# Expert choice in a three-block network: fewer candidate places, a fused look-up, and 62 pieces of the first expert layer in 512-column products

## The chip, the cores and the metric
One NeuronCore of a Trainium2 chip. The metric is the device time of one execution in microseconds (us), the median of several runs of the same program. Engines are named as in the profile: PE (TensorE matrix products), PEld (its weight loads), DVE (VectorE), ACT (ScalarE), POOL (GpSimd), SP (SyncE, which issues the loads).

## The reference, cut to what matters
The network has three blocks over 256 tokens of width 1024. The change lies in the expert layer (PEER) that ends the second block. For each token there are 8 heads; each head picks 16 of 16384 experts through two lists of 128 keys:

```python
q = (xt @ w_q).reshape(T, PEER_HEADS, PEER_QDIM)
s1 = jnp.einsum('thd,hkd->thk', q[..., :half], keys1)
s2 = jnp.einsum('thd,hkd->thk', q[..., half:], keys2)
v1, i1 = lax.top_k(s1, PEER_TOPK)
v2, i2 = lax.top_k(s2, PEER_TOPK)
cand = (v1[..., :, None] + v2[..., None, :]).reshape(T, PEER_HEADS, 256)
cidx = (i1[..., :, None] * 128 + i2[..., None, :]).reshape(T, PEER_HEADS, 256)
sv, pos = lax.top_k(cand, PEER_TOPK)
eidx = jnp.take_along_axis(cidx, pos, axis=-1)
gw = jax.nn.softmax(sv, axis=-1)
act = jnp.einsum('td,thkd->thk', xc, jnp.take(u_tab, eidx, axis=0))
hact = jax.nn.gelu(act, approximate=False) * gw
y = jnp.einsum('thk,thkd->td', hact, jnp.take(v_tab, eidx, axis=0))
```

## The kernel before, in words
The kernel gathers no rows of `u_tab`. It multiplies all 16384 rows with all 256 tokens, takes the Gelu of all products, builds a weight for every (expert, token) pair that is zero where the expert was not chosen, multiplies the two, and multiplies the result with all of `v_tab`. `peer` exists once for each engine (L1228 PE, L2419 DVE, L3504 ACT; POOL's part starts at L1496).

A **piece** is 128 rows of a weight matrix with all 1024 inputs, a tile of 128 x 1024. Each number is carried as a high part (rounded to fp32r) and a low part (the rest). SP loads a chunk of two pieces (1 MB) into one of three raw slots; ACT makes the high part of each piece (L2896), DVE (L1543) or POOL (L1431, `lower`) subtracts to get the low part. The parts lie in a ring of four, so the high part of piece n can be made when PE has read piece n-4; a raw slot is loaded again when both its pieces have their low parts. In every engine's program `weights()` steps to the next piece: ACT makes high parts up to three pieces ahead, DVE low parts up to two pieces ahead, except those listed in `on_pool` (L379), which POOL makes in a row of its own.

`peer`'s stretch of 128 pieces of `u_tab` has two stages, cut at piece `SELECTED`.

- **Search stage**, pieces 0 to 71. PE makes each piece's products in the narrow form (`tile_mms`, L580): 8 x (high weights with high inputs, high weights with low inputs) and 8 x low weights with high inputs, 24 products of 256 columns, each with its own weight load. Two pieces share a PSUM bank of the four in `main`. ACT takes the Gelu of two pieces from PSUM (L3547). DVE runs the choice of experts beside it, as a generator, `select()` (L2474), which `shared` lets go on by 1750 columns with each piece: 32 rounds of five instructions (L2453 to L2458: largest 8, their places, strike them out, next 8, their places) on 128 scores; per token half the 256 sums of 16 x 16 candidates (L2480) and eight rounds of five on 256 columns; shifts and masks that split a place into its row and column (L2487, L2489); a look-up for each of the two index lists and token halves that compares places with 0 to 15 (L2495, 2048 columns), multiplies with the indices (L2499, eight times 256 columns) and sums (L2504). ACT takes the exponential (L3560), DVE divides (L2514 to L2518). POOL makes the low part of every odd piece.
- **Weighing stage**, from piece 72. PE turns the selection around (L1259), and from piece 74 to 126, in 64 groups of four tokens, DVE, ACT and POOL build one-hot tiles (in raw slot 2, which is kept free for that), PE multiplies them into the weights (L1268), and DVE multiplies these with the Gelu (L2560) or copies them where the Gelu is not there yet (L2561). `groups_of` spreads the groups over the pieces.

The other form of product in the kernel is `wide` (L742). High and low inputs lie beside each other, so one product of 512 columns makes both parts with one weight load (L747), and 8 products of 256 columns add the low weights (L746). A piece then takes a whole bank, whose two halves are still to be added. The queries of this layer are made so: ACT copies one half (L3517), DVE adds the other (L2433).

Of the kernel before, what the change touches and what calls it, by code (L numbers as in the profile page):

```python
# [7 lines left out]
F32 = mybir.dt.float32  # L8
# [13 lines left out]
SELECTED = 72  # L22
FIRST_HOT, LAST_HOT = 74, 126
# [4 lines left out]
LOW = -3.0e38  # L28
# [263 lines left out]

BAND = [(o, i) for o in range(10) for i in range(10)
# [18 lines left out]
class Program:  # L312


    def __init__(self, nc, d, out, mem, ctx, marks, known):
# [63 lines left out]
        self.on_pool = [0] + [self.u_first + n for n in range(1, SELECTED, 2)] + [self.next_four("m3") - 1]  # L379
# [129 lines left out]
def tensor_engine(k):  # L509
# [718 lines left out]
    def peer(prev):  # L1228
# [43 lines left out]
        for n in range(128):  # L1272
            if n % 2 == 0:
                b = main.take(pe, ("pr.u", n))
            m, hi, lo = weights()
            o = n % 2 * 256
            ins = tile_mms(ps[:, b, o:o + 256], m, hi, lo, X, 0, 8, True, True, rx)
            ins.then_inc(k.piece_read, 1)
            if n % 2:
                k.full["pr.u", n - 1] = k.piece_read, m + 1  # L1280
            if n == SELECTED:
                selected()
            for g in groups_of(n):
                weigh(g)
# [132 lines left out]
def gpsimd_engine(k):  # L1417
# [80 lines left out]
    for n in range(1, SELECTED, 2):  # L1498
        lower(k.u_first + n)
# [28 lines left out]
def vector_engine(k):  # L1528
# [893 lines left out]
    def peer(prev):  # L2422
# [17 lines left out]
        pd = k.AR[:, B0 + 2048:B0 + 2560].bitcast(U32).rearrange("p (j s n) -> p j s n", s=2, n=128)  # L2440
        pf = k.AR[:, B0 + 2560:B0 + 3072].rearrange("p (j s n) -> p j s n", s=2, n=128)
        sel = k.AR[:, B0 + 3072:B0 + 3840].rearrange("p (w j n) -> p w j n", w=3, n=128)
        cand = k.AR[:, B0 + 4096:B0 + 6144].rearrange("p (h a b) -> p h a b", a=16, b=16)
        eq = k.AR[:, B0 + 6144:B0 + 8192]
        e3 = eq.rearrange("p (n a) -> p n a", a=16)
        e4 = eq.rearrange("p (h k a) -> p h k a", k=16, a=16)
# [23 lines left out]
        def select():  # L2470
# [6 lines left out]
            yield 256  # L2477
            for j in range(2):
                v.wait_ge(*k.dma["spilled"].need("x"))
                chained(te.tensor_tensor(cand, bc(v_[:, j, 0].unsqueeze(3), [128, 8, 16, 16]),  # L2480
                                         bc(v_[:, j, 1].unsqueeze(2), [128, 8, 16, 16]), ALU.add))
                yield 2048
                for h in range(8):
                    yield from best(sv[:, j, h], pu[:, j, h], cand[:, h].rearrange("p a b -> p (a b)"))
            for j in range(2):
                pj = pu[:, j].rearrange("p h k -> p (h k)")
                chained(te.tensor_single_scalar(pd[:, j, 0], pj, 4, ALU.logical_shift_right))  # L2487
                yield 128
                chained(te.tensor_single_scalar(pd[:, j, 1], pj, 15, ALU.bitwise_and))  # L2489
                yield 128  # L2490
            chained(te.tensor_copy(k.AR[:, B0 + 2560:B0 + 3072], k.AR[:, B0 + 2048:B0 + 2560].bitcast(U32)))
            yield 256
            for j in range(2):
                for sd in range(2):
                    chained(te.tensor_tensor(e3, bc(pf[:, j, sd].unsqueeze(2), [128, 128, 16]),  # L2495
                                             bc(k.iota[:, 0:16].unsqueeze(1), [128, 128, 16]), ALU.is_equal))
                    yield 2048
                    for h in range(8):
                        ins = te.tensor_tensor(e4[:, h], e4[:, h], bc(ifl[:, j, sd, h].unsqueeze(1), [128, 16, 16]),  # L2499
                                               ALU.mult)  # L2500
                        if h == 7:
                            chained(ins)
                        yield 256
                    chained(te.tensor_reduce(sel[:, sd, j], e3, AX.X, ALU.add))  # L2504
# [10 lines left out]
            yield 256  # L2515
            chained(te.reciprocal(st[:, 80:96], st[:, 64:80]))
            yield 16
            te.tensor_tensor(sel[:, 2].rearrange("p j (h k) -> p (j h) k", k=16), svn,  # L2518
                             bc(st[:, 80:96].unsqueeze(2), [128, 16, 16]), ALU.mult).then_inc(*step.mark("pr.sel"))
            yield 256  # L2520
# [32 lines left out]
        def weighed(g, m):  # L2553

            v.wait_ge(*full["pr.w", g])
            if not weighed_before(m - 2):
                v.wait_ge(*main.gone(("pr.u", m - 2)))
# [321 lines left out]
def scalar_engine(k):  # L2879
# [624 lines left out]
    def peer(prev):  # L3504
# [34 lines left out]
        def taken(f):  # L3539

            t = weighed_before(f) * 4
# [8 lines left out]
        for n in range(128):  # L3550
# [6 lines left out]
            if n == SELECTED - 2:  # L3557
                w = k.AR[:, B0 + 1536:B0 + 1792]
                a.wait_ge(*s["vec"].need(("pr.sv", 1)))
                act(w, w, ACT.Exp).then_inc(*s["act"].mark("pr.exp"))  # L3560
# [5 lines left out]
            if n % 2 and n < 127:  # L3566
                taken(n - 1)
# [379 lines left out]
```

## Time and profile before
| what | value |
|---|---|
| median of 3 runs | 2816.77 us (2816.17 to 2816.78) |
| span of the profiled execution, first to last instruction | 2814.9 us |
| what lies around the span, median less span | 1.9 us |
| busy in the span: PE, DVE, ACT, POOL | 2800.3, 1952.1, 1624.4, 345.9 us |

The page gives the profiled execution's span; its whole time is taken as one of the runs listed. How to read the rows: in the timeline the first number is the start from the span's beginning, the second the time from there to the end of the last of the instructions merged in the row, both in us; in brackets stands how long the engine was idle before it and whom it waited for. PE instructions overlap, so its pace is read from starts. A piece of the narrow form has one row of eight low-weight products (L589), one of the wide form a row of eight at L746.

### The profile page before, as it was taken

Reading aid. Unit: us, or ns where it says so; the run is one execution under the profiler, and the core shown is the slowest. Engines: PE = TensorE matmul, PEld = TensorE weight load, DVE = VectorE, ACT = ScalarE, POOL = GpSimd, SP = SyncE. Lnnn points to the kernel's source line nnn. Section 1 sums busy time; section 2 is a strip of 40 time slices with the busy share of each in tenths; the row PEclk is TensorE's granted clock in tenths of the full one; section 3 lists DMA queues with packets and bytes.
Section 4 is the critical chain, followed back from the end, with each engine's and each line's share of the span. In section 5 each row is a group of like instructions: output and inputs, shape, how many; then the busy total and the mean of one; then the engine's idle time right before and its main releaser. Section 6 shows DMA issues by size and latency. Waiting matters only on the chain.

```text
span 2814.9 us, 42397 instructions
## 1 busy us (share of the span) xinstructions
PE 2800.3 (99%) x16834; PEld 2485.0 (88%) x16834; DVE 1952.1 (69%) x3377; ACT 1624.4 (58%) x2784; POOL 345.9 (12%) x314
## 2 busy tenths in 40 slices
PE   9999999999999999999999999999999999999999
PEld 7888888888988888899889999999888889988997
DVE  6657765776676676768866998677555566766775
ACT  6544655755665564566745445776555555655663
POOL 0000000000010002000002445894000000000000
PEclk9999999999999999999999999999999999999999
DMA  7554556466436555445164554434555574536454
GB/s 229 191 178 159 181 194 227 135 202 221 148 124 194 202 189 181 135 156 187 61 224 166 183 182 160 136 131 161 193 192 193 194 246 137 180 110 209 147 195 149
DMA packets 270485, 491.25 MB, mean 175 GB/s; under 512 B 10880, under 2 KB 181248, under 8 KB 261584
## 3 DMA queue, kind: packets, MB, share of 16 engines
q1 hardware_dynamic: 268864, 480.08, 51.3%
q0 software_dynamic: 1424, 8.45, 0.8%
q8 instruction: 135, 2.21, 0.3%
q14 instruction: 62, 0.51, 0.1%
HBM read 486.41 MB, written 2.10 MB: 174 GB/s over the span
## 4 chain that ended last, share of the span: by engine, by line
PE 94%; DVE 4%; ACT 1%; issue 0%; DMA 0%; POOL 0%; DVEq 0%; POOLq 0%; ACTq 0%
PE ps L659 41%; PE ps L747 11%; PE ps L589 8%; PE ps L585 8%; PE ps L586 8%; PE ps L746 6%; PE ps L606 3%; PE ps L1268 2%; DVE halves L1543 1%; PE ps L1303 1%; PE ps L544 1%; DVE AR L2499 1%; PE ps L952 0%; PE ps L1322 0%; DVE AR L2495 0%
## 5 line engine op out<-in xcount | busy, mean ns | idle before, releaser
L2896 ACT ACTIVATE halves<-raw 128x1024 fp32r<-128x1024 f32 x828 | 870.1, 1058 | 695.5 <-PE ps L659 413.7
L1543 DVE TENSOR_TENSOR halves<-raw,halves 128x1024 fp32r<-128x1024 f32 x790 | 952.9, 1227 | 190.6 <-ACT halves L2896 187.4
L659 PE MATMUL ps<-halves,XX 128*128 128x512 f32 x2628 | 611.6, 391 | 0.4
L659 PEld LDWEIGHTS ps<-halves,XX 128*128 128x128 f32 x2628 | 489.9, 188 | 102.5 <-DVE XX L1581 1.0
L585 PE MATMUL ps<-XX,halves 128*128 128x256 f32 (+1 forms) x1960 | 486.1, 286 | 0.0
L586 PE MATMUL ps<-XX,halves 128*128 128x256 f32 (+1 forms) x1960 | 480.3, 283 | 0.0
L659 PE MATMUL ps<-halves,R 128*128 128x512 f32 x1908 | 439.9, 390 | 0.1
L659 PEld LDWEIGHTS ps<-halves,R 128*128 128x128 f32 x1908 | 356.7, 188 | 73.9 <-issue 0.6
L586 PEld LDWEIGHTS ps<-XX,halves 128*128 128x128 f32 (+1 forms) x1960 | 375.4, 192 | 0.1
L585 PEld LDWEIGHTS ps<-XX,halves 128*128 128x128 f32 (+1 forms) x1960 | 375.0, 191 | 0.1
L747 PE MATMUL ps<-XX,halves 128*128 128x512 f32 x1344 | 338.4, 393 | 0.6 <-DVE XX L1581 0.6
L747 PEld LDWEIGHTS ps<-XX,halves 128*128 128x128 f32 x1344 | 241.7, 189 | 44.5 <-ACT halves L2896 0.9
L589 PE MATMUL ps<-XX,halves 128*128 128x256 f32 (+1 forms) x1960 | 275.3, 283 | 0.2 <-DVE halves L1543 0.2
L589 PEld LDWEIGHTS ps<-XX,halves 128*128 128x128 f32 (+1 forms) x1960 | 252.7, 192 | 0.4 <-DVE halves L1543 0.4
L746 PEld LDWEIGHTS ps<-XX,halves 128*128 128x128 f32 x1344 | 183.2, 190 | 13.4 <-issue 0.4
L746 PE MATMUL ps<-XX,halves 128*128 128x256 f32 x1344 | 187.5, 282 | 0.1
L1426 POOL TENSOR_TENSOR st<-st 128x1 f32<-128x1 f32 x44 | 25.3, 574 | 1182.0 <-DVE st L1608 1001.9
L1431 POOL TENSOR_TENSOR halves<-raw,halves 128x1024 fp32r<-128x1024 f32 x38 | 97.0, 2552 | 435.3 <-ACT halves L2896 435.3
L1558 DVE TENSOR_TENSOR XX<-AR,XX 128x256 fp32r<-128x256 f32 x127 | 53.9, 426 | 137.9 <-ACT XX L3579 137.9
L1509 POOL TENSOR_SCALAR raw<-iota,xsel 128x128 f32<-128x128 f32 x128 | 137.5, 1081 | 34.5 <-PE ps L1268 22.4
L1807 DVE TENSOR_TENSOR AR<-AR,ps 128x256 f32<-128x256 f32 x164 | 68.5, 421 | 81.1 <-ACT AR L3096 81.1
L3096 ACT ACTIVATE AR<-ps 128x256 f32<-128x256 f32 x164 | 61.3, 375 | 89.4 <-PE ps L747 88.0
(390 smaller groups left out, 3180.8 us busy)
## 6 DMA issues: line engine op xcount, KB each, us to landing
raw<-in_w_ffn_in SPq DMA_DIRECT2D x88, 1024.0 KB, 5.1
raw<-in_w_in SPq DMA_DIRECT2D x74, 1024.0 KB, 5.3
raw<-in_uT SPq DMA_DIRECT2D x64, 1024.0 KB, 4.9
raw<-in_peer_v SPq DMA_DIRECT2D x64, 1024.0 KB, 4.9
raw<-in_w_ffn_out SPq DMA_DIRECT2D x44, 1024.0 KB, 4.9
raw<-in_w_up SPq DMA_DIRECT2D x24, 1024.0 KB, 5.8
raw<-in_mlstm_w_in SPq DMA_DIRECT2D x12, 1024.0 KB, 5.2
raw<-in_w_down SPq DMA_DIRECT2D x12, 1024.0 KB, 4.9
```

Of the source, the lines that this page charges most:

```text
L585: mm(o[:, ts], hi[:, q, 0:M], xh[:, k0 + q, ts], start=first and q == 0, stop=False)
L586: mm(o[:, ts], hi[:, q, 0:M], xl[:, k0 + q, ts], start=False, stop=False)
L589: ins = mm(o[:, ts], lo[:, q, 0:M], xh[:, k0 + q, ts], start=False, stop=last and q == a - 1)
L606: ins = mm(ps[:, bs[j], :].rearrange("p (a b) -> p a b", b=128), act[q == 2][:, t, j * 128:(j + 1) * 128], k.halves[:, 0:4, q % 2, t * 128 ...
L659: ins = mm(ps[:, bs[j * (width // 512) + h], :], xv[:, k0 + t, j * 128:(j + 1) * 128], wv[:, t, h * 512:(h + 1) * 512], start=first and q ...
L746: mm(o[:, 0:256], lo[:, p, :], X[0][:, p, :], start=False, stop=False)
L747: ins = mm(o.rearrange("p (h t) -> p h t", t=256), hi[:, q, :], k.XX[:, :, q, :], start=q == 0, stop=q == 7)
L1431: nc.gpsimd.tensor_tensor(lo, src, hi.bitcast(F32), ALU.subtract).then_inc(k.lo_pool, 1)
L1509: nc.gpsimd.tensor_scalar(OA[:, g % 2, q, :], k.iota[:], ih1[:, 4 * g + q:4 * g + q + 1], gw[:, 4 * g + q:4 * g + q + 1], ALU.is_equal, AL ...
L1543: te.tensor_tensor(lo, src, hi.bitcast(F32), ALU.subtract).then_inc(k.lo_made, 1)
L1807: te.tensor_tensor(dst, dst, o[:, 0:256], ALU.add) \
L2896: act(hi, src, ACT.Copy).then_inc(k.hi_made, 1)
```

## The change
- The top 16 of 16 x 16 sums of two sorted lists can lie in few places only: `select` now forms 64 of them in four blocks (row 0 with 16 columns, rows 1 to 3 with 8, rows 4 to 7 with 4, rows 8 to 15 with 1), behind 8 places of filler, 72 columns a head. Row and column of a place are worked out by shifts, maxima and minima.
- The look-up compares and multiplies in one instruction (is_equal, then mult) for each of 16 rows and each token half, 256 columns; four sums of 2048 stay.
- Pieces 0 to 61 use `wide`, each with a bank of its own; DVE adds the bank's halves with one TENSOR_REDUCE into SBUF, one piece behind PE; ACT's Gelu works in SBUF on two pieces, four behind.
- `SELECTED` goes from 72 to 62, the first weighing group from piece 74 to 64, the step of `shared` from 1750 to 1600 columns. The end of the selection (`shares`) leaves the generator; the exponential moves from piece `SELECTED - 2` to `SELECTED - 1`.
- POOL makes the low part of pieces with n odd or n % 8 == 2, in four instructions of 256 columns.

```diff
-SELECTED = 72
-FIRST_HOT, LAST_HOT = 74, 126
+SELECTED = 62
+FIRST_HOT, LAST_HOT = 64, 126
...
+def low_on_pool(n):
+    return n % 2 == 1 or n % 8 == 2
...
-        for n in range(128):
+        for n in range(SELECTED):
+            wide(("pr.u", n), main, rx)
+        for n in range(SELECTED, 128):
...
-    def lower(n):
+    def lower(n, step=8):
         src, hi, lo = k.piece(n)
         gp.wait_ge(k.hi_made, n + 1)
-        nc.gpsimd.tensor_tensor(lo, src, hi.bitcast(F32), ALU.subtract).then_inc(k.lo_pool, 1)
+        for q in range(0, 8, step):
+            ts = slice(q, q + step) if step < 8 else slice(None)
+            ins = nc.gpsimd.tensor_tensor(lo[:, ts], src[:, ts], hi[:, ts].bitcast(F32), ALU.subtract)
+        ins.then_inc(k.lo_pool, 1)
...
-    for n in range(1, SELECTED, 2):
-        lower(k.u_first + n)
+    for n in range(SELECTED):
+        if low_on_pool(n):
+            lower(k.u_first + n, 2)
...
-                chained(te.tensor_tensor(cand, bc(v_[:, j, 0].unsqueeze(3), [128, 8, 16, 16]),
-                                         bc(v_[:, j, 1].unsqueeze(2), [128, 8, 16, 16]), ALU.add))
-                yield 2048
+                for at, a0, a, b in ((8, 0, 1, 16), (24, 1, 3, 8), (48, 4, 4, 4), (64, 8, 8, 1)):
+                    o = cand[:, j, :, at:at + a * b].rearrange("p h (a b) -> p h a b", b=b)
+                    ins = te.tensor_tensor(o, bc(v_[:, j, 0, :, a0:a0 + a].unsqueeze(3), [128, 8, a, b]),
+                                           bc(v_[:, j, 1, :, 0:b].unsqueeze(2), [128, 8, a, b]), ALU.add)
+                    if at == 64:
+                        chained(ins)
+                    yield 8 * a * b
...
+            chained(te.tensor_scalar(pa, pw[:, 1], -2.0, 0.0, ALU.add, ALU.max))
+            chained(te.scalar_tensor_tensor(pa, pw[:, 2], -8.0, pa, ALU.add, ALU.max))
...
+                for a in range(16):
+                    ins = te.scalar_tensor_tensor(eq[:, a].rearrange("p (r k) -> p r k", k=16), pj, float(a),
+                                                  bc(ij[:, :, a:a + 1], [128, 16, 16]), ALU.is_equal, ALU.mult)
...
+        def shares():
             v.wait_ge(*s["act"].need("pr.exp"))
...
-        v.begin(shared(select(), 1750), 1)
+        v.begin(shared(select(), 1600), 1)
         for n in range(128):
             if n == SELECTED:
                 v.finish()
+                shares()
             weights()
+            if 1 <= n <= SELECTED:
+                v.wait_ge(*full["pr.u", n - 1])
+                b = main.of(("pr.u", n - 1))
+                te.tensor_reduce(act[:, n - 1, :], ps[:, b, :].rearrange("p (h t) -> p t h", t=256), AX.X, ALU.add) \
+                    .then_inc(*main.done(("pr.u", n - 1)))
...
+            if f < SELECTED:
+                a.wait_ge(*main.gone(("pr.u", f + 1)))
+                act(hidden[:, f:f + 2, :], hidden[:, f:f + 2, :], ACT.Gelu).then_inc(*s["act"].mark(("pr.h", f)))
+                return
...
+            if n == SELECTED - 1:
+                w = k.AR[:, B0 + 1536:B0 + 1792]
+                a.wait_ge(*s["vec"].need(("pr.sv", 1)))
+                act(w, w, ACT.Exp).then_inc(*s["act"].mark("pr.exp"))
+            if n % 2 == 0 and 4 <= n <= SELECTED:
+                taken(n - 4)
```

## Rows read from the trace of the kernel before
**Rows 1.** The page: chain that ended last, by engine; low halves on DVE
```profile
PE 94%; DVE 4%; ACT 1%; issue 0%; DMA 0%; POOL 0%; DVEq 0%; POOLq 0%; ACTq 0%
...
L1543 DVE TENSOR_TENSOR halves<-raw,halves 128x1024 fp32r<-128x1024 f32 x790 | 952.9, 1227 | 190.6 <-ACT halves L2896 187.4
```
**Rows 2.** The search stretch: us, then PE, PEld, DVE, ACT, POOL busy, clock, DMA share, GB/s
```profile
1520.00:1727.00 207.00, 206.84 (x1723) 206.57 (x1722) 188.72 (x474) 97.31 (x112) 89.37 (x35) 1.00 0.52 174
```
**Rows 3.** Timeline of PE, queries in the wide form, four pieces in a row
```profile
1502.82 1.12 PE L746 MATMUL ps<-XX,halves 128*128 128x256 f32 x8
...
1511.20 1.12 PE L746 MATMUL ps<-XX,halves 128*128 128x256 f32 x8
```
**Rows 4.** Timeline of PE, search stage in the narrow form, two pieces in a row
```profile
1524.70 1.12 PE L589 MATMUL ps<-XX,halves 128*128 128x256 f32 x8
...
1527.58 1.12 PE L589 MATMUL ps<-XX,halves 128*128 128x256 f32 x8
```
**Rows 5.** Timeline of PE, weighing stage: one group between the first two, then two
```profile
1747.41 1.12 PE L589 MATMUL ps<-XX,halves 128*128 128x256 f32 x8
...
1751.18 1.12 PE L589 MATMUL ps<-XX,halves 128*128 128x256 f32 x8
...
1756.06 0.76 PE L589 MATMUL ps<-XX,halves 128*128 128x256 f32 x5
```
**Rows 6.** Timeline of DVE, first instruction of the search
```profile
1520.73 0.29 DVE L2453 MAX8 AR<-AR 128x8 f32<-128x128 f32 x1 [6.17 <-ACT AR L3523]
```
**Rows 7.** DVE by line and form, 1520.7 to 1726.7: busy us, mean ns, idle before
```profile
L2453 DVE MAX8 AR<-AR 128x8 f32<-128x128 f32 x64 | 18.9, 295 | 8.2 <-ACT AR L3523 6.2
...
L2453 DVE MAX8 AR<-AR 128x8 f32<-128x256 f32 x32 | 13.7, 427 | 0.9
```
**Rows 8.** The same view, instructions that POOL can hold up
```profile
L1543 DVE TENSOR_TENSOR halves<-raw,halves 128x1024 fp32r<-128x1024 f32 x35 | 47.8, 1365 | 6.7 <-ACT halves L2896 6.2
L2499 DVE TENSOR_TENSOR AR<-AR 128x256 f32<-128x256 f32 x32 | 22.2, 755 | 0.0
...
L2495 DVE TENSOR_TENSOR AR<-AR,iota 128x2048 f32<-128x2048 f32 x4 | 11.3, 2816 | 0.1
...
L2480 DVE TENSOR_TENSOR AR<-AR 128x2048 f32<-128x2048 f32 x2 | 4.6, 2292 | 0.1
...
L2476 DVE CAST AR<-AR 128x512 f32<-128x512 uint32 x1 | 2.3, 2259 | 0.0
...
L2491 DVE CAST AR<-AR 128x512 f32<-128x512 uint32 x1 | 0.4, 426 | 0.0
```
**Rows 9.** Timeline of DVE, four products in a row; last instruction of the selection
```profile
1716.88 1.42 DVE L2499 TENSOR_TENSOR AR<-AR 128x256 f32<-128x256 f32 x4
...
1726.35 0.42 DVE L2518 TENSOR_TENSOR AR<-AR,st 128x256 f32<-128x256 f32 x1
```
**Rows 10.** Waits of DVE, 1520.7 to 1726.7: us in total, times, longest
```profile
DVE halves L1543 <- ACT halves L2896: 6.2, 15, 0.9
DVE st L2514 <- ACT AR L3560: 2.8, 1, 2.8
```
**Rows 11.** Timeline of DVE, 512 columns copied out of PSUM
```profile
1731.53 0.69 DVE L2528 COPY xsel<-ps 128x512 f32<-128x512 f32 x1 [0.21 <-PE ps L1259]
1732.13 0.41 DVE L2529 COPY xsel<-ps 128x256 f32<-128x256 f32 x1
```
**Rows 12.** Timeline of POOL and of DVE, two low halves at one time
```profile
1677.24 2.41 POOL L1431 TENSOR_TENSOR halves<-raw,halves 128x1024 fp32r<-128x1024 f32 x1 [3.12 <-ACT halves L2896]
...
1677.76 2.97 DVE L1543 TENSOR_TENSOR halves<-raw,halves 128x1024 fp32r<-128x1024 f32 x1
```
**Rows 13.** POOL by line and form, whole span: busy us, mean ns, idle before
```profile
L1426 POOL TENSOR_TENSOR st<-st 128x1 f32<-128x1 f32 x44 | 25.3, 574 | 1182.0 <-DVE st L1608 1001.9 <-DVE st L1629 173.9 <-DVE st L2814 6.3
```
**Rows 14.** Timeline of PE, a late low half
```profile
1711.90 0.28 PE L586 MATMUL ps<-XX,halves 128*128 128x256 f32 x1
1712.34 0.74 PE L589 MATMUL ps<-XX,halves 128*128 128x256 f32 x4 [0.16 <-DVE halves L1543]
```

More of the change, by code:

```diff
@@ L378, in __init__ @@
         self.u_first = self.last_piece[u - 1]
-        self.on_pool = [0] + [self.u_first + n for n in range(1, SELECTED, 2)] + [self.next_four("m3") - 1]
+        self.on_pool = [0] + [self.u_first + n for n in range(SELECTED) if low_on_pool(n)] + [self.next_four("m3") - 1]
         self.slot, self.loads, self.before = [], [], []
@@ L2477, in select @@
             yield 256
+            v.wait_ge(*k.dma["spilled"].need("x"))
+            chained(te.memset(cand[:, :, :, 0:8], LOW))
+            yield 128
             for j in range(2):
-                v.wait_ge(*k.dma["spilled"].need("x"))
-                chained(te.tensor_tensor(cand, bc(v_[:, j, 0].unsqueeze(3), [128, 8, 16, 16]),
-                                         bc(v_[:, j, 1].unsqueeze(2), [128, 8, 16, 16]), ALU.add))
-                yield 2048
-                for h in range(8):
-                    yield from best(sv[:, j, h], pu[:, j, h], cand[:, h].rearrange("p a b -> p (a b)"))
@@ new lines, in select @@
+                for h in range(8):
+                    yield from best(sv[:, j, h], pu[:, j, h], cand[:, j, h])
+            pn = pu.rearrange("p j h k -> p j (h k)")
+            chained(te.tensor_single_scalar(place[:, 0], pn, 3, ALU.logical_shift_right))
+            yield 256
+            chained(te.tensor_single_scalar(place[:, 1], pn, 2, ALU.logical_shift_right))
+            yield 256
+            te.tensor_copy(pw[:, 0], pn)
+            yield 256
+            chained(te.tensor_copy(pw[:, 1:3], place))
@@ new lines, in select @@
+            yield 512
+            pa, pb, q0, q1 = pf[:, :, 0], pf[:, :, 1], eq[:, 0].rearrange("p (j n) -> p j n", n=128), \
+                eq[:, 1].rearrange("p (j n) -> p j n", n=128)
+            chained(te.tensor_scalar(pa, pw[:, 1], -2.0, 0.0, ALU.add, ALU.max))
+            chained(te.scalar_tensor_tensor(pa, pw[:, 2], -8.0, pa, ALU.add, ALU.max))
+            yield 512
+            chained(te.scalar_tensor_tensor(pa, pw[:, 0], -56.0, pa, ALU.add, ALU.max))
+            te.tensor_scalar(q1, pa, 4.0, 24.0, ALU.mult, ALU.add)
@@ L2492, in select @@
+            yield 512
+            chained(te.tensor_scalar(q0, pa, 8.0, 8.0, ALU.mult, ALU.add))
+            chained(te.scalar_tensor_tensor(q0, pa, 16.0, q0, ALU.mult, ALU.min))
+            yield 512
+            chained(te.tensor_tensor(q0, q0, q1, ALU.min))
+            chained(te.scalar_tensor_tensor(q0, pa, 48.0, q0, ALU.add, ALU.min))
+            yield 512
+            chained(te.scalar_tensor_tensor(pb, pw[:, 0], -8.0, q0, ALU.add, ALU.subtract))
             yield 256
             for j in range(2):
-                for sd in range(2):
[L2495 to L2504, printed above, removed]
@@ new lines, in select @@
+                pj = pf[:, j].rearrange("p s (h k) -> p (s h) k", k=16)
+                ij = ifl[:, j].rearrange("p s h k -> p (s h) k")
+                for a in range(16):
+                    ins = te.scalar_tensor_tensor(eq[:, a].rearrange("p (r k) -> p r k", k=16), pj, float(a),
+                                                  bc(ij[:, :, a:a + 1], [128, 16, 16]), ALU.is_equal, ALU.mult)
+                    if a == 15:
+                        chained(ins)
+                    yield 256
@@ L3565, in peer @@
                 a.wait_ge(*full["pr.s", 1, 1, 4])
-            if n % 2 and n < 127:
+            if n == SELECTED - 1:
[4 more added lines that the diff above has]
+                taken(n - 4)
+            if n == SELECTED + 1:
+                taken(SELECTED - 2)
+            if n % 2 and SELECTED < n < 127:
                 taken(n - 1)
```

27 lines of the change are left out of this document (7 added, 20 removed).

## Prediction
> **What bounds the kernel now.** I read the page's chain of waits first: PE stands in 94% of it [rows 1], so a change pays only where PE gets less to do or waits less. Then the stretches: while the experts are searched (1520 to 1727 us) PE is busy 206.84 of 207 us and DVE 188.72 [rows 2]; DVE is the engine with the least room beside PE, and the one to which this change gives work. The PE timeline gives the period of a piece: 2.880 us in the old form, from one low-half group to the next [rows 4]; 2.793 in the form with 512 columns, which this kernel already runs for the queries (8.38 us for three pieces) [rows 3]. Last, the DVE rows of the stretch, to see what its time consists of [rows 6 to 9]. The durations are of one profiled execution, whose span is 2814.9 us [rows 1]; the median of the runs, 2816.8, is 1.9 above it for what lies outside first and last instruction. I carry that over and forecast on the median.
>
> **What PE gains.** 62 pieces x (2.880 - 2.793) = 5.4 us: weights are loaded 16 times instead of 24, and both periods are of PE running without a gap. The 64 weighing groups spread over 62 pieces instead of 52. A piece with one group takes 3.77, with two 4.88 [rows 5], so a second group costs 1.11 where the first costs 0.89; of twelve such pieces six show this 0.22 (the others 4.66). Two such pieces remain: between 0.9 and 1.3, I take 1.1. Finally PE waits for a late low half before the products of piece 66: 0.44 instead of 0.12 [rows 14], and 0.1 more at piece 62 in the same way; 0.4 goes, if DVE is not late there again. Together 6.9 us.
>
> A rule speaks against this term. The Trainium skill (TensorE: Matmul & The Clock Gate, section Back-to-back issue gap) gives N/2.4 + 2.5 ns for a matmul alone. By it a piece is 24 x 109 = 2.62 us before and 8 x 216 + 8 x 109 = 2.60 after, and the 62 pieces give back an estimated 1.2 us instead of 5.4. The rows have 120 ns and 230 ns in place of its 109 and 216, so they decide here.
>
> **What DVE must do in the same stretch.** Before, it goes from the first search instruction at 1520.73 [rows 6] to the end of the weights at 1726.77 [rows 9]: 206.0 us, of which 6.2 + 2.8 are waits for ACT [rows 10]; 197.0 of work. Some of that is being held up by POOL: the low half at 1677.76 takes 2.97 instead of 1.23 and ends 1.08 after POOL's instruction from 1677.24 has ended at 1679.65 [rows 12]. Summed over the groups by their means: 35 x (1365 - 1227) = 4.8, 32 x (755 - 414) = 10.9, 4 x (2816 - 2292) = 2.1, 2259 - 426 = 1.8 [rows 8]; 414 ns is the product when not held up, (1.42 - 0.41)/3 = 0.34 apart [rows 9]. That is 19.6, which leaves 177.4. The edits, start to start:
> - 80 second-level search instructions on 72 columns instead of 256: 1.04 ns a column, from 427 - 295 ns over 128 columns [rows 7], so 80 x 0.191 = -15.3.
> - Two candidate sums of 2.33 [rows 8] become eight of 64 to 192 columns, together 1024/2 columns x 2 tokens: about 1.8. -2.9.
> - Look-up: the four comparisons over 2048 columns go (-9.3), the 32 products stay as 32 fused instructions of the same two inputs and width; the four sums stay.
> - Place arithmetic: five instructions (shifts, masks, a cast) become fourteen, nine more; the widest now, 512 columns, takes 0.43 [rows 8], most are half as wide. At 0.29 each: +2.6.
> - Low halves: POOL takes five of eight instead of four; with ten pieces fewer 24 instead of 34 stay on DVE, 10 x 1.14 = -11.4.
> - The new sum out of PSUM: no row has it. Nearest is the 512-column copy out of PSUM, 0.69, the next instruction 0.60 after it [rows 11]. Lower end 0.53 (512 x 1.04), upper 1.2 if each half were read at half rate; I take 0.60, since a sum of 256 columns has the fixed part of a copy. 61 x 0.60 = +36.6 (range +32 to +73).
>
> 177.4 - 15.3 - 2.9 - 9.3 + 2.6 - 11.4 + 36.6 = 177.7, and 2.8 for the exponential, which still needs DVE's last numbers first: 180.5 us without any hold-up. PE comes to the turning of the selection after 62 x 2.793 + 2.88 = 176.0 from 1519.82, which is 175.1 after 1520.73. **DVE is 5.4 us short.** Before it had the time of 72 pieces of 2.88, and 9 us of waiting to spare.
>
> **Hold-ups.** They don't vanish. POOL held its inputs 2.41 of every 5.76 us, 42%; now five pieces in eight, in quarters of 256 columns. A quarter costs at least 0.60 (2.41/4). The only dearer neighbour is POOL's instruction on one column, 574 ns [rows 13], by which a quarter is 0.574 + (2.41 - 0.574)/4 = 1.03. In 8 x 2.793 = 22.3 us that is 20 x 0.60 = 12.0 (54%) to 20.6 (92%). DVE has some 77 instructions that meet it (24 low halves, 32 look-ups, 8 + 13 small ones); each waits half a quarter on average: 77 x 0.54 x 0.30 = 12.5, to 77 x 0.92 x 0.52 = 37. I take 12.5: 2.41 is the same operation, the other one is a power. Nothing in the rows excludes fewer, so the low end is 0.
> The Trainium skill (GPSIMD Engine Reference, section 3.1) has 4497 ns for 2048 columns; with 2.41 for 1024 that is an estimated 0.83 a quarter, and the sum would give some 24 us of hold-ups instead of 12.5.
>
> **What waits.** PE takes a bank for piece n only when DVE has summed piece n-4, and needs low half n; so DVE may be about 8 us behind (three pieces of 2.79 less its own 0.6) before PE stops, first near piece 25, then at DVE's pace, and once more at the selection. Behind DVE's new wait for PE stand its low halves and the search. On ACT the Gelu, now from SBUF after DVE's sum (0.60 before, out of PSUM), has the next high halves behind it; ACT is busy 97.31 of 207 [rows 2] and that is cover as long as DVE is less than some 6 us behind. SP gets a raw slot back with the low halves, so loads move with DVE too; five of eight come from POOL. Raw slot 2 is taken away ten pieces sooner, which costs nothing where loads run two deep now without a stall. In the weighing stage DVE is busy 141.20 and POOL 173.06 of 195 [rows 2], with groups now further apart: cover for the same groups.
>
> Sum: 2816.8 - 6.9 + 5.4 + 12.5 = **2827.8 us**, slower.
>
> **Rivals.**
> 1. DVE keeps pace (faster). The hold-ups stay near zero because a quarter lets DVE in at once, and the sum out of PSUM costs 0.53, -4.3 us. It decides where DVE's stretch falls below 176.4: 2816.8 - 6.9 = 2809.9. For it: the searching instructions, a third of the time, show no hold-up at all. Against it: 177.7 has no slack in it, and every stretch with look-ups shows hold-ups. 0.18.
> 2. DVE short, but hardly held up (no change): 5.4, or a few us more, against 6.9: 2815.3, up to 2822. For it: a blocked instruction now waits for a quarter at most. 0.22.
> 3. POOL is the bound: at 1.03 a quarter it is busy 20.6 of 22.3 us, and DVE's own instructions push it over: 37 of hold-ups, 2816.8 - 6.9 + 5.4 + 37 = 2852. 0.07.
> 4. The 512-column form does not reach 2.793 here. It runs in the same kernel with the same operands; 0.02, and then only the 5.4 is lost (inside the other cases).
>
> **Numbers.** Forecast 0.53. A measurement of this kernel tells about 0.2% (5.6 us) from no change, so 2811.1 to 2822.4 is "same". The forecast's own range is 2816 to 2838 (hold-ups 0 to 23); four parts in five of it are slower by more than 0.2%, with rival 3 and the top of rival 2 that is about 0.58; same 0.23; faster 0.19. The range must reach to rival 1: 2809 to 2836 leaves out rival 3 and the forecast's tail.
>
> **What the new profile would show.** Right: piece periods of 2.79 up to about piece 25 and longer after, PE released by DVE's new sum and by the end of the selection, DVE without idle time up to there, POOL quarters of 0.6 to 0.9, 3.77 for nearly every weighing piece. Wrong: PE periods of 2.79 through piece 61 (rival 1), or DVE idle waiting for PE before the selection ends; a sum out of PSUM much off 0.6; POOL without idle time (rival 3).

## The result, and the profile after

The changed kernel takes **2834.39 us** (median, 2833.51 to 2834.49), the one before 2816.71 beside it: ratio 1.0061, 95% interval 1.0049 to 1.0074. It is 17.7 us slower. The profiled execution spans 2832.7 us, 1.7 under the median.

The page's chain and the search stretch, against [rows 1, 2] (columns of the second fence: stretch, us, then busy time of PE, PEld, DVE, ACT, POOL, clock, DMA share, GB/s):

```profile
PE 88%; DVE 9%; ACT 2%; issue 1%; DMA 0%; POOL 0%; SPq 0%; DVEq 0%; POOLq 0%
```
```profile
1520.00:1727.00 207.00, 189.12 (x1074) 163.83 (x1073) 195.41 (x543) 90.99 (x105) 123.16 (x152) 0.98 0.45 158
```
PE stood in 94% of the chain and now in 88%; DVE went from 4 to 9%. In the stretch PE has 17.9 us without work where it had 0.2, and DVE is busy 195.41 of 207. PE's waits from 1515 to 1730 (us in total, times, longest), and then DVE's and two of ACT's, against [rows 10]:

```profile
PE ps L752 <- DVE AR L2604: 14.1, 12, 2.6
PE ps L1264 <- DVE AR L2551: 2.5, 1, 2.5
PE ps L590 <- DVE AR L2604: 1.3, 1, 1.3
...
DVE AR L2463 <- ACT AR L3561: 7.3, 1, 7.3
DVE halves L1554 <- ACT halves L2934: 2.5, 2, 1.9
...
ACT AR L3581 <- DVE AR L2604: 40.2, 21, 5.9
ACT AR L3607 <- DVE AR L2542: 5.3, 1, 5.3
```
PE waits 14 times, each time for DVE: 13 times for a bank that the new sum (L2604) has not read, once for the finished selection. DVE waits for nobody inside the stretch: its 7.3 lie before its first search instruction and its 2.5 behind the selection. So DVE sets the end. ACT's Gelu (L3581) waits 40.2 us for DVE as well, but no wait of PE names ACT: that cover held.

Where it starts, in PE's timeline, against [rows 3, 4]; the last two lines are the end of the stage:

```profile
1521.28 1.11 PE L751 MATMUL ps<-XX,halves 128*128 128x256 f32 x8
...
1524.07 1.12 PE L751 MATMUL ps<-XX,halves 128*128 128x256 f32 x8
...
1608.71 1.86 PE L752 MATMUL ps<-XX,halves 128*128 128x512 f32 x7 [0.52 <-DVE AR L2604]
...
1614.15 0.39 PE L752 MATMUL ps<-XX,halves 128*128 128x512 f32 x1
1616.90 3.31 PE L752 MATMUL ps<-XX,halves 128*128 128x512 f32 x7 [2.35 <-DVE AR L2604]
...
1716.60 1.12 PE L594 MATMUL ps<-XX,halves 128*128 128x256 f32 x8
1720.19 0.87 PE L1264 MATMUL ps<-ident,AR 128*128 128x128 f32 x6 [2.48 <-DVE AR L2551]
```
From one piece's low-half products to the next piece's it is 2.79 at first. From piece 20 on (2.93, then 3.23 from piece 22, 3.87 from 24) some periods are longer, up to 6.82 from piece 32. Had all 62 stayed at 2.793, piece 62 would have come to its low-half products near 1694.8 (61 periods, and 3.10 from the last wide piece to the first narrow one, as in the last run below); it comes at 1716.60, 21.8 later, and 2.5 more go at the turning of the selection: 24.3 late. The waits are 17.9 of this; the rest lies behind them, some 0.2 at each restart and some 3 where PE's clock was lower (last section). Less the 6.9 that PE gains by the forecast's own terms that is 17.4, and 17.7 was measured.

What DVE does in 1520 to 1722, by line and form (busy us, mean ns | idle before), against [rows 7, 8]:

```profile
L2604 DVE TENSOR_REDUCE AR<-ps 128x256 f32<-128x512 f32 x62 | 42.7, 690 | 1.8
L1554 DVE TENSOR_TENSOR halves<-raw,halves 128x1024 fp32r<-128x1024 f32 x26 | 34.7, 1333 | 0.0
...
L2530 DVE SCALAR_TENSOR_TENSOR AR<-AR 128x256 f32<-128x256 f32 x32 | 16.5, 572 | 0.0
L2536 DVE TENSOR_REDUCE AR<-AR 128x128 f32<-128x2048 f32 x4 | 15.3, 3816 | 0.1
...
L2463 DVE MAX8 AR<-AR 128x8 f32<-128x72 f32 x32 | 7.5, 235 | 0.9
...
L2494 DVE TENSOR_TENSOR AR<-AR 128x128 f32<-128x128 f32 x4 | 2.7, 670 | 0.0
L2494 DVE TENSOR_TENSOR AR<-AR 128x192 f32<-128x192 f32 x2 | 1.8, 892 | 0.0
L2494 DVE TENSOR_TENSOR AR<-AR 128x64 f32<-128x64 f32 x2 | 1.5, 749 | 0.0
...
L2515 DVE SCALAR_TENSOR_TENSOR AR<-AR 128x256 f32<-128x256 f32 x1 | 0.8, 848 | 0.0
```
And POOL's quarters in the same stretch, against [rows 12]:

```profile
L1440 POOL TENSOR_TENSOR halves<-raw,halves 128x256 fp32r<-128x256 f32 x148 | 120.2, 845 | 68.9 <-ACT halves L2934 68.9
```
The sum out of PSUM takes 690 ns, the time of the copy of as many columns [rows 11]. The row that nobody expected is L2536: each of the four look-up sums takes 3816 ns. In the kernel before, from 1520.7 to 1726.7, the same sum took

```profile
L2504 DVE TENSOR_REDUCE AR<-AR 128x128 f32<-128x2048 f32 x4 | 9.1, 2283 | 0.1
```
Three rows of 64 to 192 columns that take 670 to 892 ns are short instructions held up by POOL (229 to 352 ns in the run below that all but takes POOL away).

### The profile page after: what moved, and what is told of

Its sections match the earlier page's. It is cut to its first block, busy times and chain, and to the rows that moved or that the text cites. A ratio compares the mean times of both kernels' runs of the same rounds, so it can differ in the third digit from the quotient of the medians.

```text
span 2832.7 us, 41646 instructions
## 1 busy us (share of the span) xinstructions
PE 2801.3 (99%) x16338; PEld 2460.6 (87%) x16338; DVE 1965.4 (69%) x3452; ACT 1626.5 (57%) x2789; POOL 394.7 (14%) x434
## 4 chain that ended last, share of the span: by engine, by line
PE 88%; DVE 9%; ACT 2%; issue 1%; DMA 0%; POOL 0%; SPq 0%; DVEq 0%; POOLq 0%
PE ps L664 40%; PE ps L752 11%; PE ps L594 6%; PE ps L590 6%; PE ps L591 6%; PE ps L751 6%; PE ps L611 3%; PE ps L1273 2%; DVE halves L1554 1%; DVE AR L2604 1%; DVE AR L2465 1%; DVE AR L2463 1%; PE ps L1310 1%; DVE AR L2530 1%; PE ps L549 1%
## 5 line engine op out<-in xcount | busy, mean ns | idle before, releaser
L752 PE MATMUL ps<-XX,halves 128*128 128x512 f32 x1840 | 468.6, 395 | 14.8 <-DVE AR L2604 14.1
L752 PEld LDWEIGHTS ps<-XX,halves 128*128 128x128 f32 x1840 | 332.4, 190 | 78.1 <-issue 17.9
L590 PE MATMUL ps<-XX,halves 128*128 128x256 f32 (+1 forms) x1464 | 365.2, 287 | 1.3 <-DVE AR L2604 1.3
L591 PE MATMUL ps<-XX,halves 128*128 128x256 f32 (+1 forms) x1464 | 358.6, 283 | 0.0
L590 PEld LDWEIGHTS ps<-XX,halves 128*128 128x128 f32 (+1 forms) x1464 | 279.6, 191 | 1.7 <-DVE AR L2604 1.6
L591 PEld LDWEIGHTS ps<-XX,halves 128*128 128x128 f32 (+1 forms) x1464 | 280.0, 191 | 0.1
L751 PEld LDWEIGHTS ps<-XX,halves 128*128 128x128 f32 x1840 | 251.5, 191 | 18.8 <-issue 0.4
L751 PE MATMUL ps<-XX,halves 128*128 128x256 f32 x1840 | 257.1, 283 | 0.1
L594 PE MATMUL ps<-XX,halves 128*128 128x256 f32 (+1 forms) x1464 | 205.5, 283 | 0.0
L594 PEld LDWEIGHTS ps<-XX,halves 128*128 128x128 f32 (+1 forms) x1464 | 188.8, 192 | 0.0
L1440 POOL TENSOR_TENSOR halves<-raw,halves 128x256 fp32r<-128x256 f32 (+1 forms) x158 | 131.0, 861 | 384.5 <-ACT halves L2934 384.5
L1520 POOL TENSOR_SCALAR raw<-iota,xsel 128x128 f32<-128x128 f32 x128 | 158.3, 1245 | 54.6 <-PE ps L1273 33.8
```

The costliest lines, as they stand in the source:

```text
L590: mm(o[:, ts], hi[:, q, 0:M], xh[:, k0 + q, ts], start=first and q == 0, stop=False)
L591: mm(o[:, ts], hi[:, q, 0:M], xl[:, k0 + q, ts], start=False, stop=False)
L594: ins = mm(o[:, ts], lo[:, q, 0:M], xh[:, k0 + q, ts], start=False, stop=last and q == a - 1)
L751: mm(o[:, 0:256], lo[:, p, :], X[0][:, p, :], start=False, stop=False)
L752: ins = mm(o.rearrange("p (h t) -> p h t", t=256), hi[:, q, :], k.XX[:, :, q, :], start=q == 0, stop=q == 7)
L1440: ins = nc.gpsimd.tensor_tensor(lo[:, ts], src[:, ts], hi[:, ts].bitcast(F32), ALU.subtract)
```

## The experiments

The theory after this reading: DVE's own work plus POOL's hold-ups is longer than the 62 pieces, and the four sums make it longer by 6.1 us (4 x (3816 - 2283), the latter what the same sum took before) because a sum's 16 terms now lie 1024 bytes apart. Rivals: the new sum out of PSUM is the cause by itself; POOL's 148 quarters are.

**Adjacent terms.** The products are written so that the 16 terms of a sum are neighbours (`en` and `es` are views of the buffer of `eq` with the 16 terms innermost).

```diff
-  te.scalar_tensor_tensor(eq[:, a].rearrange("p (r k) -> p r k", k=16), pj, float(a), ...
+  te.scalar_tensor_tensor(en[:, :, :, a], pj, float(a), ...
-  te.tensor_reduce(sel[:, sd, j], eq[:, :, sd * 128:sd * 128 + 128].rearrange("p a n -> p n a"), ...
+  te.tensor_reduce(sel[:, sd, j], es[:, sd * 128:sd * 128 + 128, :], ...
```


> The changed kernel with the look-up's products stored so that the 16 terms of one sum lie next to each other (they lay 1024 bytes apart); the products are then written 64 bytes apart. DVE theory (DVE's amount of work up to the turned selection sets the time): the four sums fall from 3.82 to about 2.29 us as before, DVE has 6.1 us less, and the time falls by as much, to about 2828.3, unless the products get dearer. Bank theory (PE waits because a piece needs a whole bank of four, a matter of hand-over, not of DVE's sum of work): under 2 us. POOL theory (late low halves from POOL set the pace): no change.

Measured 2834.47, ratio to before 1.0062 (1.0046 to 1.0079): nothing gained, a miss. The DVE rows by form:

```profile
L2532 DVE SCALAR_TENSOR_TENSOR AR<-AR 128x256 f32<-128x256 f32 x32 | 22.3, 808 | 0.0
L2538 DVE TENSOR_REDUCE AR<-AR 128x128 f32<-128x2048 f32 x4 | 9.1, 2282 | 0.1
```
The sums are down to 2282 ns as expected, 6.2 us less of busy time (15.3 before this edit); the 32 products rose from 16.5 to 22.3 us, 5.8 more. (Their means, 572 and 808 ns, overlap where one product follows another, so the busy time is the price.) Two causes are possible: the products are now written 64 bytes apart, or POOL, which ran beside the long sums, now meets the products.

The selection ends 2.4 us sooner in this trace, at 1717.71, and the profiled execution, at 2832.99 the shortest of four, is 1.4 under the changed kernel's median. Part of the 2.4 was lost right behind the turning of the selection, in PE's timeline:

```profile
1717.77 1.52 PE L1264 MATMUL ps<-ident,AR 128*128 128x128 f32 x6 [2.47 <-DVE AR L2553]
...
1721.95 1.12 PE L594 MATMUL ps<-XX,halves 128*128 128x256 f32 x8
```
From the turning to these low-half products it takes 4.18 us, in the changed kernel 2.63 (1720.19 to 1722.82): the granted clock was 0.64 from 1717 to 1720 and 0.69 from 1720 to 1722. Some 0.6 came back at a later group, where PE no longer waits for ACT. So the one trace shows a gain of DVE of which the clock ate a part; why the other three executions, at 2834.36 to 2834.93, gained nothing stays open.

**POOL all but taken away.** POOL's low halves are cut to 16 of 1024 columns; the kernel leaves out the rest of the low parts that POOL makes.

```diff
+        if step < 8:
+            lo, src, hi = lo[:, 0:1, 0:16], src[:, 0:1, 0:16], hi[:, 0:1, 0:16]
+        ins = nc.gpsimd.tensor_tensor(lo, src, hi.bitcast(F32), ALU.subtract)
```


> The changed kernel in which POOL makes only 16 of the 1024 columns of each of its low halves in the search stage; the rest of these low halves is left out (old contents are multiplied). POOL's time in the stretch is nearly gone, DVE's and PE's instructions are the same. DVE theory: what is saved are the hold-ups, 24 x 0.13 on low halves, 32 x 0.155 on look-ups, some 3.7 on the candidate sums and 4 on the place arithmetic, together about 16: about 2819. Bank theory: a few us at most. POOL theory: PE is no longer held, near 2810.

Measured 2819.54, ratio 1.0009 (0.9999 to 1.0018), as the theory had it. POOL's hold-ups are worth 14.9 us, and without them the products take 416 ns and the low halves 1219; but PE still waits for DVE, and the kernel still isn't the 6.9 us faster that PE gains:

```profile
PE ps L752 <- DVE AR L2604: 3.8, 5, 2.1
PE ps L1264 <- DVE AR L2551: 2.5, 1, 2.5
...
L2536 DVE TENSOR_REDUCE AR<-AR 128x128 f32<-128x2048 f32 x4 | 15.3, 3836 | 0.1
L2530 DVE SCALAR_TENSOR_TENSOR AR<-AR 128x256 f32<-128x256 f32 x32 | 11.6, 416 | 0.0
```

**Both together.** The same two edits in one kernel, with the same part left out.

> Two edits together: the look-up's terms lie side by side (each sum of 16 then reads adjacent numbers) and POOL makes 16 of the 1024 columns of its low halves. This kernel leaves out most of the low parts that POOL makes. POOL's hold-ups are gone, as in the run with the sliver alone (2819.5), so VectorE's time is its own work. If the four sums cost 6.1 us more in the changed kernel for the stride of their terms, and the run with adjacent terms gained nothing only because the freed time went into hold-ups, this run is 4 to 6 us faster than the sliver alone: 2813.5 to 2815.5. If the stride of the sums never was on the path, it stays at 2819.5.

Measured 2816.14, ratio 0.9998 (0.9989 to 1.0007): 3.4 under the sliver alone (2.6 between the two profiled executions), just outside the range, but on the theory's side. Four products in a row show what is missing; first this kernel, then the sliver alone:

```profile
1659.72 1.98 DVE L2532 SCALAR_TENSOR_TENSOR AR<-AR 128x256 f32<-128x256 f32 x4
...
1670.67 2.29 DVE L2538 TENSOR_REDUCE AR<-AR 128x128 f32<-128x2048 f32 x1
```
```profile
1659.90 1.42 DVE L2530 SCALAR_TENSOR_TENSOR AR<-AR 128x256 f32<-128x256 f32 x4
...
1668.91 3.89 DVE L2536 TENSOR_REDUCE AR<-AR 128x128 f32<-128x2048 f32 x1
```
Start to start, a product takes (1.42 - 0.41)/3 = 0.34 us when it writes neighbours and (1.98 - 0.58)/3 = 0.47 when it writes 64 bytes apart (0.41 and 0.58 are the last one's own time). So the layout itself takes back 32 x 0.13 = 4.2 us of the 6.1; 1.9 are left, and 3.4 were measured.

```profile
L2532 DVE SCALAR_TENSOR_TENSOR AR<-AR 128x256 f32<-128x256 f32 x32 | 16.2, 621 | 0.0
```
By busy time the 32 products cost 16.2 - 11.6 = 4.6 us more here, and 5.8 more in the first run, with POOL at work: longer hold-up is only 1.2 us of that run. The selection ends 2.6 us sooner here than with the sliver alone (1701.85 and 1704.44) and ended 2.4 sooner there. So adjacent terms free some 2.5 us of DVE's time with and without POOL, not 6.1, because the products pay for them.

**POOL's low halves whole.** `lower(k.u_first + n)` in place of `lower(k.u_first + n, 2)`: one instruction of 1024 columns.

> The changed kernel with POOL's low halves in one instruction of 1024 columns (2.4 us) instead of four of 256 (3.4 us together). DVE theory with hold-ups: POOL holds less in all (36 x 2.4 = 86 us instead of 36 x 3.4 = 122) but an instruction that meets it waits for up to 2.4 instead of 0.84; before, 19.6 us of hold-ups came from 42% of POOL, now its share is about 50%, so some 20 to 30 instead of 16: 4 to 14 us slower, 2838 to 2848. POOL theory: POOL has 36 us less to do, so the time falls clearly, below 2825.

Measured 2842.73, ratio 1.0093 (1.0076 to 1.0109), inside the range. The quarters are a gain of 8.3 us against whole halves, though POOL is busy less with these (37 of 2567 ns, 94.9 us, against 120.2). In that trace DVE's low halves take 1563 ns instead of 1333, its products 672 instead of 572.

**The narrow form.** The search's pieces in 24 products of 256 columns again, ACT taking the Gelu out of PSUM, no sum on DVE; all else as changed.

```diff
-        for n in range(SELECTED):
-            wide(("pr.u", n), main, rx)
-        for n in range(SELECTED, 128):
+        for n in range(128):
```


> The changed kernel with the search pieces in the narrow form again, two to a bank, Gelu straight out of PSUM, no sum on DVE; candidates, look-up, POOL's share and the cut at 62 stay. DVE theory: DVE's stretch is 199.6 - 61 x 0.60 = 163 us against PE's 62 x 2.88 + 2.88 = 181, so PE is the bound: 2816.7 less 1.1 for fewer doubled groups and 0.4 for the late low halves, about 2815.2. POOL theory, or one in which the raw slots or the look-up by itself cost the time: still near 2834.

Measured 2822.53, ratio 1.0020 (1.0011 to 1.0030), a miss by 7 us. PE waits only twice, in the last piece and at the selection, while DVE had been idle for 16.6 us before:

```profile
PE ps L594 <- DVE halves L1552: 2.4, 1, 2.4
PE ps L1264 <- DVE AR L2549: 2.4, 1, 2.4
...
DVE halves L1552 <- ACT halves L2927: 16.6, 14, 2.6
```
Behind the second wait PE is slow, as in the run with adjacent terms (granted clock 0.50 from 1706 to 1709, 0.58 from 1709 to 1711; 4.35 us from the turning to the next low-half products instead of 2.63). So it was not work but **pace**: the choice counts 98,718 columns in all (each instruction's own and 170), and at 1600 a piece that is 61.7 pieces of 62. The same kernel with a step of 1800:

> The search stage in the narrow form again, so no sum out of PSUM on VectorE; only the step of `shared` goes from 1600 to 1800 columns a piece, so that the choice is through near piece 55 instead of 61. The theory that VectorE's own work is the bound says: with the narrow form VectorE's stretch is some 163 us (199.6 less 61 sums at 0.60) against the 178.6 us that TensorE gives it, so the 2822.5 of the run with the old step was a matter of pace: the choice came out in the last piece. With the new step TensorE no longer waits before the turning of the selection, and the time is the before's less the 1.5 us of late low halves and doubled groups: 2815.2 (2813.5 to 2817). The rival, that what is left of the choice (look-up in quarters, the slower sums) costs time wherever it stands, says 2822 again.

Measured 2815.49, ratio 0.9995 (0.9986 to 1.0004). No wait of PE is left, and DVE still waits 12.3 us for ACT's high halves. The two waits and the slow clock behind them, 4.8 and 1.7, are most of the 7.0 us between the two runs. This settles that without the sums out of PSUM DVE has time enough, and it isolates the two small gains of PE: 1.2 us against the 1.5 of the forecast.

**The cut at 72 alone.** `SELECTED = 72`, groups from 74, and with it a step of 1400, since the same choice has ten more pieces.

> The changed kernel with the cut at piece 72 instead of 62 (groups from 74, step 1400), nothing else: TensorE gets 10 more pieces of 2.79 us in the search stage, and VectorE 10 more sums (6.0) and 4 more low halves (4.6). VectorE's stretch is then about 199.6 + 10.6 = 210 us, and TensorE reaches the turning of the selection 203 us after the first search instruction: still 7 us late instead of 24, of which 6.3 + 0.4 come back from the 72 wide pieces, but 1.1 of the doubled groups is lost. Theory (VectorE is short of time, and the cut at 62 made it so): 2815 to 2819. Rival (the hold-ups grow with the number of pieces, since POOL runs with TensorE and VectorE only fills what is left): 10 more pieces bring nothing, 2830 or more.

Measured 2816.43, ratio 0.9999 (0.9990 to 1.0008), as expected: with ten more pieces of time for the same choice the time is that of before. PE still waits 4.7 us for the sum and 0.2 for the selection.

**ACT takes one half.** ACT copies one half of the bank to SBUF, DVE adds the other; cut at 72, step 1500.

```diff
-                v.wait_ge(*full["pr.u", n - 1])
+                v.wait_ge(*s["beside"].need(("pr.u", n - 1)))
...
-                te.tensor_reduce(act[:, n - 1, :], ps[:, b, :].rearrange("p (h t) -> p t h", t=256), AX.X, ALU.add) \
+                te.tensor_tensor(act[:, n - 1, :], act[:, n - 1, :], ps[:, b, 0:256], ALU.add) \
...
+            if 1 <= n <= SELECTED:
+                a.wait_ge(*full["pr.u", n - 1])
+                act(hidden[:, n - 1, :], ps[:, main.of(("pr.u", n - 1)), 256:512], ACT.Copy) \
+                    .then_inc(*s["beside"].mark(("pr.u", n - 1)))
```


> The cut at 72 (step 1500), and the two halves of a bank added as for the queries: ScalarE copies one half out of PSUM, VectorE adds the other, an instruction of 256 columns (0.35 to 0.45 us) in place of the sum of 512 (0.60 to 0.69). VectorE's stretch is about 210 less 72 times 0.25 = 192 us against the 203 that TensorE gives, so VectorE is no longer the bound. Theory: 2816.7 less 72 times 0.087 (6.3) less 0.4 = 2810 (2808.5 to 2812.5), below both kernels. Rival: ScalarE's 72 more copies stand between its high halves and make them late, or TensorE waits for the slower chain of two engines at each bank: 2816 or more, with waits of TensorE on ScalarE's high halves.

Measured 2815.62, ratio 0.9994 (0.9986 to 1.0003): a miss by 5 us. DVE's instruction is down to 419 ns, but PE waits 4.1 us for two banks, both behind a pair of look-up sums. DVE's timeline at the first:

```profile
1676.22 3.83 DVE L2536 TENSOR_REDUCE AR<-AR 128x128 f32<-128x2048 f32 x1
1680.08 0.76 DVE L2604 TENSOR_TENSOR AR<-AR,ps 128x256 f32<-128x256 f32 x2
1680.75 3.90 DVE L2536 TENSOR_REDUCE AR<-AR 128x128 f32<-128x2048 f32 x1
```
`shared` counts such a sum as 2218 columns, one and a half pieces of 1500. That is 4.1 us of PE's time, but DVE owes some 0.34 for the addition and 0.43 for low halves in each piece, which leaves an estimated 3.0; the sum takes 3.83. I read the 13.1 us that DVE waited for ACT in this run as slack in the early pieces and set the pace higher.

**A faster pace: three runs.** A step of 1800, each look-up product counted as 640 columns; then adjacent terms as well; then the cut at 68.

> As the run with ScalarE copying one half and the cut at 72, with another pace only: the step of `shared` from 1500 to 1800 columns, and each look-up product counted as 640 columns instead of 256, near what it takes when POOL holds it up (730 to 930 ns). In that run VectorE waited 13.1 us for ScalarE's copies in the early pieces and was late by two banks (4.1 us) where two look-up sums of 3.8 us stand close together. Theory (pace: VectorE has time enough, but takes the choice too slowly at first and too fast in the look-up): TensorE waits under 2 us, 2811.5 to 2813.5. Rival (the sums of 3.8 us are longer than a piece wherever they fall): the two bank waits stay, 2814.5 to 2816.

> The same and the look-up's terms side by side, so that a sum takes 2.28 us, less than the 2.79 of a piece, instead of 3.82. Theory: no bank is late, VectorE's stretch is some 190 us plus up to 8 of longer products against 203, and only the 72 x 0.087 + 0.4 = 6.7 of TensorE's own gain is left: 2810 (2809 to 2811.5). Rival (the products written 64 bytes apart are held up as much longer as the sums are shorter, and the choice ends as late as before): 2814 to 2816.

> The same with the cut at 68 (first group from 70): 4 x 0.087 = 0.35 us less from the wide form, and groups spread over four more pieces, so some four doubled ones fewer, 4 x 0.11 to 0.22 = 0.4 to 0.9 back. The choice, at 111,000 counted columns and 1800 a piece, is through in piece 62. Theory: 2809.5 (2808.5 to 2811). Rival (the choice is not through before piece 68, as at 62): TensorE waits at the turning of the selection, 2813 or more.

Measured 2819.90, 2818.94 and 2820.10 (ratios 1.0011 (1.0002 to 1.0020), 1.0005 (0.9996 to 1.0014) and 1.0011 (1.0001 to 1.0020)): all three missed, and PE's waits are where neither theory had them. PE's waits in the first two runs, and DVE's in the second:

```profile
PE ps L752 <- DVE AR L2604: 7.0, 10, 1.7
```
```profile
PE ps L752 <- DVE AR L2606: 6.5, 9, 1.7
...
DVE AR L2606 <- ACT AR L3612: 18.2, 9, 3.0
```
PE is late in pieces 22 to 40, in the search, and DVE idle at the end, from 1706 on (in the third run PE waits 6.6 us in the same pieces). My premise was wrong: of the 13.1 us only 3.9 lay in the early pieces (seven waits up to 1591), 9.2 came after 1714, when the choice was through. DVE had next to nothing to spare in the search.

**The pace in between.** Adjacent terms, ACT's half, cut at 72, a step of 1560, a product counted as 500.

> As the run with ScalarE's half, adjacent terms and the cut at 72, but with a step of 1560 instead of 1800 columns and a look-up product counted as 500 instead of 640. At 1800 TensorE was late in pieces 22 to 40, in the search, by about 9 us, and VectorE idle for 18 us at the end; at 1500 it was not late there, but in the look-up. Counted from these two, VectorE needs 2.65 us a piece in the search at 1500 and 3.2 at 1800, so about 2.75 at 1560, against 2.79; in the look-up 1560/670 = 2.3 products of 0.94 plus 0.33 and 0.43 are 2.95, a lag of under 2 us in eight pieces, of 8 that the banks allow. The choice, at 106,500 counted columns, is through in piece 68. Theory (pace): no bank is late, 2816.9 less 72 x 0.087 and 0.4 = 2810.2 (2809 to 2812). Rival (the lag builds up wherever the choice meets POOL, whatever the step): 6 us and more of waits stay, 2815 or more.

Measured **2809.91** (2809.59 to 2810.71), ratio to before 0.9976 (0.9966 to 0.9985): as expected, and under both kernels. The search stretch, and DVE's waits:

```profile
1520.00:1720.00 200.00, 200.00 (x1145) 175.72 (x1145) 184.14 (x545) 115.59 (x179) 139.32 (x172) 1.00 0.52 180
```
```profile
DVE AR L2606 <- ACT AR L3612: 7.6, 8, 3.0
```
PE is busy for the whole of the stretch. The 6.8 us gained against before are PE's own terms: 72 x 0.087 + 0.4 = 6.7. Whether the same pace would do with the long sums, or with DVE's sum of both halves, wasn't tried.

## Why the prediction was right, and where it was off

**The course was right.** The kernel is slower, by DVE, which is late from the twenties on and stops PE at banks and once more at the selection. The loss was forecast as 11.0 us and is 17.7. It is a lack of DVE time, and no one instruction's fault: without the sums out of PSUM, without most of POOL's work, or with ten more pieces the kernel is back within 3 us of before. The forecast's stretch for DVE was 180.5 + 12.5 = 193.0 us; it was 199.6, from 1520.49 to the last instruction of the selection, which stands against [rows 9] as

```profile
1719.71 0.42 DVE L2551 TENSOR_TENSOR AR<-AR,st 128x256 f32<-128x256 f32 x1
```
With the 6.6 us between the two the sum would have been 2834.4, the time measured. Step by step:

- **"The four sums stay"** is the step that failed. They stayed in number and width, not in cost: 3816 ns instead of 2283, +6.1 us. The code shows it: the reduced axis was the innermost before and is now the outermost of the buffer (the line taken out in the first run's diff). I took the price from the row of an instruction of the same name and shape; the row has neither the stride of its input nor that of its output. Adjacent terms show the size, 2282 ns, and that the layout must be paid on one side or the other: of the 6.1 us only some 2.5 could be had back.
- **Hold-ups**: 12.5 forecast; 14.9 by the run with the sliver, and 15.8 added up from the rows of the changed kernel less those of that run (low halves 26 x 114 ns = 3.0, products 32 x 156 = 5.0, candidate sums 3.7, nine of the place arithmetic 4.1). The size came out near for a poor reason: a quarter takes 0.845, not the 0.60 I took, and with 0.845 my own formula gives 77 x 0.76 x 0.42 = 24.6. POOL was in fact busy for 120.2 us of 202, 0.60 and not 0.76, because the stretch got longer; with that the formula gives 19. The 77 instructions wait 0.21 on average (0.54 x 0.30 = 0.16 forecast, 0.60 x 0.42 = 0.25 by the formula with both numbers right): POOL is in the way more than I took, and less of an instruction's time goes when it is.
- **The rest of DVE's work** is some 2.8 us less than forecast (6.6 is 6.1 + 3.3 - 2.8). That is the size of the term for the exponential, 2.8, and this wait is gone: DVE's waits above have none for the exponential in the stretch, where [rows 10] had 2.8. The sum out of PSUM is 0.61 from start to start (0.60 forecast), the second-level search 235 ns against 427 (0.192 each, 0.191 forecast).
- **PE's gain** stands: 1.2 of 1.5 us for late halves and doubled groups, and 6.8 against 6.7 where DVE is out of the way. Nearly all weighing pieces take 3.77. DVE and POOL, with room in that stage before, still have it; 195 us of before (the prediction's 141.20 and 173.06 stand here), then of after:

```profile
1745.00:1940.00 195.00, 195.00 (x1652) 194.10 (x1652) 141.20 (x313) 148.59 (x340) 173.06 (x181) 1.00 0.40 134
```
```profile
1765.00:1960.00 195.00, 195.00 (x1658) 194.85 (x1657) 136.30 (x286) 143.16 (x316) 162.92 (x157) 1.00 0.41 141
```

The rule of the Trainium skill (TensorE: Matmul & The Clock Gate, Back-to-back issue gap), by which the wide form would give back an estimated 1.2 us for 62 pieces, is stated there for a product alone, and is not what the runs show: by it the last run would have gained some 1.8 us, and it gained 6.8. The Trainium skill's price for POOL (GPSIMD Engine Reference, section 3.1), from which I estimated 0.83 a quarter (the line through its 4497 ns and the 2.41 us gives an estimated 0.845), agrees with the 0.845 measured; the 24 us of hold-ups that I worked out with it were not seen.

The rivals: DVE doesn't keep pace (1), POOL has 68.9 us to spare in 202 and its quarter is under 1.03 (3), the wide form reaches 2.79 (4). Rival 2, hardly any hold-up, falls by the 14.9 us. The upper end, 2836, held the time because the hold-ups had been given up to 23 us, not because anything allowed for the sums: that part is luck. Two slips of the prediction decide nothing. Rival 1's bound of 176.4 should be the 175.1 that the sum before it has for PE, and rival 1's own terms miss it (180.5 - 4.3 = 176.2). And since all of rival 2 lies within "same", the chances add up to about 0.49 slower and 0.33 same, not 0.58 and 0.23.

## What to carry to other kernels

Work that runs beside a matmul stream has a budget per piece, and a cut that shortens the stream takes from it: here ten pieces less and a sum per piece turned 9 us of slack into a lack. When a layout changes, price every instruction that reads or writes it anew. And when side work is paced by a count, check the count against time in each of its parts: at a step of 1500 PE was late in the look-up, at 1800 in the search, and at 1560 (with shorter sums and dearer counted products) nowhere.

## What the runs showed of the hardware

- **VectorE pays for strides in SBUF, in both directions.** 2048 columns summed over 16 neighbours take 2.28 us, over 16 terms 1024 bytes apart 3.82. A product of 256 columns takes 0.34 us when it writes neighbours, 0.47 when it writes 64 bytes apart. Out of PSUM no such price shows: the sum of two halves 1024 bytes apart takes 0.69 us, the plain copy of 512 columns 0.68 in the same trace. The Trainium skill (SBUF — State Buffer, in Door 1: The DMA port swizzle) tells of 16-byte lines, where each access that goes on to a new line costs more; both SBUF figures agree with that in kind.
- **POOL holds up some DVE instructions and not others.** The long sums and the searching instructions take the same with POOL's quarters and with its slivers (2282 and 2282 ns; 235 and 235), products and low halves don't (572 and 416; 1333 and 1219). The Trainium skill (SBUF — State Buffer, Who interferes with whom) says that an instruction with two inputs in SBUF meets GpSimd's reads and a reduction never does: the trace agrees.
- **TensorE's clock fell behind some of the waits, not all.** After the one of 2.35 us shown above, seven products take 3.31 us instead of 1.86, and the stretch has a granted clock of 0.58, so for part of it PE was at 1.2 instead of 2.4 GHz:

```profile
1612.00:1616.00 4.00, 2.55 (x15) 1.98 (x14) 3.93 (x7) 0.86 (x1) 4.00 (x5) 1.00 0.49 160
1616.00:1620.00 4.00, 3.10 (x7) 2.48 (x8) 3.69 (x18) 1.58 (x2) 1.03 (x2) 0.58 0.76 248
...
1706.00:1710.00 4.00, 1.66 (x12) 1.26 (x10) 3.97 (x2) 0.00 (x0) 0.00 (x0) 1.00 0.75 262
1710.00:1714.00 4.00, 3.04 (x16) 2.45 (x16) 3.97 (x3) 2.87 (x3) 0.00 (x0) 1.00 0.00 0
```
The same happens near 1671 (0.66), but not after the longest wait, 2.60 us before 1710.26. At the turning of the selection it fell in the run with adjacent terms, behind a wait of 2.47 us, and not in the changed kernel, behind one of 2.48. What decides was not tried. In the search of the changed kernel it should have cost nothing, because DVE, which set the pace, waited for no product; behind the turning, in the run with adjacent terms, it cost time: 4.18 us instead of 2.63.
